# Recurrent convolution read from PSUM, separate counts for its two readers, and statistics products at other places

## What is computed

```
x_new = layer_norm(DEEPNORM_ALPHA * x + gate[:, None] * y, ln_g, ln_b)
...
h = rms_norm(x, g_mix_pre[l])
z = h @ w_in[l]
...
# rg_lru_branch(xb, gb): xb = u_rx, gb = u_rg, both 1024 x 1024 columns of z
xc = causal_dwconv(xb, conv_w, conv_b)            # 4 taps, per channel
gates = einsum('bshi,ghij->gbshj', xh, w_gates)   # 16 heads of 64, two gates
r, i = sigmoid(gates[0]), sigmoid(gates[1])
a = exp(-LRU_C * r * softplus(-lru_lambda))
u = sqrt(1 - a*a) * i * xc
h[t] = a[t] * h[t-1] + u[t]                       # over the tokens
out = h * gelu(gb)
```

## Time and profile before

| | us |
|---|---|
| median of 3 timed runs (3225.26 to 3228.08) | 3226.74 |
| the profiled execution | 3221.17 |
| its span, first to last instruction | 3219.0 |
| PE busy | 3083.0 |
| DVE, ACT, POOL busy | 1525.1, 749.5, 1187.0 |

### The profile page before, as it was taken

One profiled execution on the slowest core, in us unless ns is written; L12 is line 12 of the kernel. 1 busy time (PEld: TensorE's weight loads), 2 busy tenths in 40 slices (PEclk: granted clock), 3 DMA queues, 4 the chain that ended last, 5 costly groups with the idle time before them and its releaser, 6 DMA issues.

```text
span 3219.0 us, 40660 instructions
## 1 busy us (share of the span) xinstructions
PE 3083.0 (96%) x16864; PEld 2493.3 (77%) x16864; DVE 1525.1 (47%) x1728; ACT 749.5 (23%) x995; POOL 1187.0 (37%) x553
## 2 busy tenths in 40 slices
PE   6999998999999999899988999999899999999998
PEld 5877876788877787787666788788688888888877
DVE  3134418528643324835666602443664155155477
ACT  2011215312231123512444411112211001001132
POOL 2232220126643232047553344353244344443442
PEclk9999999999999999999999999999999999999999
DMA  6210111333231011213411111112211111111211
GB/s 245 72 33 8 35 41 48 112 127 120 72 128 33 14 41 48 73 52 105 137 53 33 40 46 51 40 53 103 77 47 46 53 46 52 46 46 52 106 44 72
DMA packets 64283, 213.39 MB, mean 66 GB/s; under 512 B 6160, under 2 KB 7952, under 8 KB 64144
## 3 DMA queue, kind: packets, MB, share of 16 engines
q1 hardware_dynamic: 44256, 149.97, 14.2%
q10 hardware_dynamic: 19888, 61.39, 5.2%
HBM read 194.56 MB, written 16.78 MB: 66 GB/s over the span
## 4 chain that ended last, share of the span: by engine, by line
PE 65%; issue 13%; DVE 11%; POOL 6%; DMA 3%; ACT 2%; POOLq 0%; SPq 0%; DVEq 0%; ACTq 0%
PE ps L586 57%; DVE Sb L2033 3%; POOL w_hi L506 3%; DMA raw<-s 3%; POOL w_lo L508 3%; PE ps L897 2%; DVE C L2353 1%; PE ps L807 1%; PE ps L722 1%; PE ps L813 0%; DVE g_lo L2435 0%; PE ps L1109 0%; PE ps L829 0%; PE ps L784 0%; DVE st L2035 0%
## 5 line engine op out<-in xcount | busy, mean ns | idle before, releaser
L506 POOL TENSOR_TENSOR w_hi<-raw,pool_zero 128x1024 fp32r<-128x1024 f32 (+2 forms) x256 | 485.1, 1895 | 1936.6 <-PE ps L586 1798.3
L508 POOL TENSOR_TENSOR w_lo<-raw,w_hi 128x1024 fp32r<-128x1024 f32 (+2 forms) x256 | 667.1, 2606 | 20.1
L586 PE MATMUL ps<-g_hi,w_hi 128*128 128x512 f32 x1632 | 535.4, 399 | 27.3 <-ACT xb L1261 11.1
L586 PE MATMUL ps<-g_lo,w_hi 128*128 128x512 f32 x1632 | 524.7, 393 | 0.0
L586 PE MATMUL ps<-g_hi,w_lo 128*128 128x512 f32 x1632 | 524.3, 392 | 0.0
L586 PE MATMUL ps<-h_hi,w_hi 128*128 128x512 f32 (+1 forms) x1496 | 429.0, 378 | 6.6 <-POOL w_lo L508 4.6
L586 PE MATMUL ps<-h_lo,w_hi 128*128 128x512 f32 (+1 forms) x1496 | 409.5, 365 | 0.0
L586 PE MATMUL ps<-h_hi,w_lo 128*128 128x512 f32 (+1 forms) x1496 | 409.1, 365 | 0.0
L586 PEld LDWEIGHTS ps<-g_hi,w_hi 128*128 128x128 f32 x1632 | 308.9, 190 | 105.6 <-ACT xb L1261 12.8
L586 PEld LDWEIGHTS ps<-g_hi,w_lo 128*128 128x128 f32 x1632 | 309.7, 190 | 65.5
L586 PEld LDWEIGHTS ps<-g_lo,w_hi 128*128 128x128 f32 x1632 | 309.5, 190 | 65.7 <-issue 1.2
(11 more groups left out here) (353 smaller groups left out, 3538.0 us busy)
## 6 DMA issues: line engine op xcount, KB each, us to landing
raw<-s SPq DMA_DIRECT2D x239, 512.0 KB, 3.4
modring<-modw ACTq DMA_DIRECT2D x32, 512.0 KB, 4.7
modfirst<-modw SPq DMA_DIRECT2D x4, 1024.0 KB, 18.0
modfirst<-modw ACTq DMA_DIRECT2D x4, 1024.0 KB, 25.0
x_saved<-Y ACTq DMA_DIRECT2D x1, 4096.0 KB, 13.4
x_part<-x_saved ACTq DMA_DIRECT2D x2, 2048.0 KB, 9.6
x_saved<-Y ACTq DMA_DIRECT2D x2, 2048.0 KB, 8.9
B<-x_saved ACTq DMA_DIRECT2D x1, 4096.0 KB, 15.6
```

What stands on the lines that cost most here:

```text
L506: G.tensor_tensor(w_hi[s][:, :n], raw[s][:, :n], zero.to_broadcast([P, n]), ALU.add).then_inc(hi_done, 1)
L508: G.tensor_tensor(w_lo[s][:, :n], raw[s][:, :n], w_hi[s][:, :n].bitcast(F32), ALU.subtract)\
L586: last = T.matmul(ps[:, o + c0:o + c0 + size], wt[s][:, kk], xx[:, k, t0:t0 + size], start=(x == 0 and n == 0), stop=(x == k_n - 1 and n = ...
```

## The change

Seven edits:

1. `convolved(c)` for c = 0 and 3 to 7 reads the slab from PSUM banks 0 and 1: the newest tap first over all 1024 columns, then the three others on shifted, shorter views. Chunks 1 and 2 still go through `xb1` and `xb2`. `xb` and the copies into it are gone.
2. DVE's order is `gated_input(c)`, `recurred(c)`, `convolved(c + 2)`, `low(c)`.
3. GELU has its own semaphore `gelu_done`. In the recurrent branch an even slab waits for `rnn_xc` and an odd slab for `gelu_done` (argument `taken`) in place of the common count; `evac_done` jumps by 16 at the first gate of the mix to be in step again.
4. The first half of chunk 0's input stays in bank 0 (no `head(0)`), S0 goes to bank 1 beside it, S2 to bank 4; the six head slabs use banks 0, 3, 1, 3, 1, 3.
5. The gate maps stand at other places: those of chunk 0 after k-step 1 of S3 (4 before), of 1 after 0 of S6 (4), of 2 after 6 of S7 (1 of S8), of 3 after 5 of S9 (6), of 4 where they were (4 of S11), of 5 after 3 of S13 (2), of 6 after 3 of S15 (7 of S14), of 7 after 1 of M1 (4 of M0).
6. The statistics products stand at other k-steps.
7. `residual(h, 0)` writes its result to the sum in PSUM too, so that n = 1 adds to PSUM; `mix_inverse(0)` goes ahead of `residual(1, 5)`.

The core of the diff (left out: the declaration of the semaphore, the ACT order's full list):

```diff
+HEAD_BANK = [0, 3, 1, 3, 1, 3]
...
                 for n in range(KD):
                     slab(G_OUT_B + n, n % 2, g_hi, g_lo, KD, half[1], 3,
-                         between=at_points(n, 0, [(0, 2), (2, 6), (3, 3), (6, 2), (7, 1)]))
+                         between=at_points(n, 0, [(0, 2), (2, 2), (3, 0), (5, 5), (6, 2)]))
                 for c in range(R_HEAD):
                     slab(G_RHEAD + c, c % 2, g_hi, g_lo, KD, half[0], 3, SPLITS["h2a"] if c == 0 else None,
-                         between=at_points(c, 1, [(0, 5), (2, 7), (3, 4), (5, 5), (5, 7)]))
+                         between=at_points(c, 1, [(0, 4), (2, 6), (3, 2), (5, 4)]), bank=HEAD_BANK[c],
+                         freed=G_RHEAD + c - 2 if c > 1 else None)
+                mix_spread(1)
...
-            first_pair(G_RNN, g_hi, g_lo, "h2b", 2, segs=(half[1], half[1]), dead=2, freed=G_RNN - 1)
-            for c in range(2, R_HEAD):
-                slab(G_RNN + c, c % 2, g_hi, g_lo, KD, half[1], 2, between=rnn_gate_maps(0, 4) if c == 3 else None)
-            gate_maps_in = {6: (1, 4), 8: (2, 1), 9: (3, 6), 11: (4, 4), 13: (5, 2), 14: (6, 7)}
+            first_pair(G_RNN, g_hi, g_lo, "h2b", 2, segs=([(512, 512, 512)], half[1]), dead=3, freed=G_RNN - 1)
+            slab(G_RNN + 2, 0, g_hi, g_lo, KD, half[1], 2, freed=G_RNN - 1, bank=4)
+            slab(G_RNN + 3, 1, g_hi, g_lo, KD, half[1], 2, between=rnn_gate_maps(0, 1), taken=(gelu_done, 1))
+            slab(G_RNN + 4, 0, g_hi, g_lo, KD, half[1], 2, taken=(rnn_xc, 1))
+            slab(G_RNN + 5, 1, g_hi, g_lo, KD, half[1], 2, taken=(gelu_done, 2))
+            gate_maps_in = {6: (1, 0), 7: (2, 6), 9: (3, 5), 11: (4, 4), 13: (5, 3), 15: (6, 3)}
             for c in range(R_HEAD, 16):
                 slab(G_RNN + c, c % 2, g_hi, g_lo, KD, SEC, 2,
-                     between=rnn_gate_maps(*gate_maps_in[c]) if c in gate_maps_in else None)
+                     between=rnn_gate_maps(*gate_maps_in[c]) if c in gate_maps_in else None,
+                     taken=(gelu_done, c // 2) if c % 2 else (rnn_xc, c // 2) if c > 6 else (evac_done, G_RNN + 1))
             for j in range(4):
-                slab(G_RMIX + 4 * j, 0, g_hi, g_lo, KD, SEC, 2, between=rnn_gate_maps(7, 4) if j == 0 else None)
-                slab(G_RMIX + 4 * j + 1, 1, g_hi, g_lo, KD, SEC, 2)
+                slab(G_RMIX + 4 * j, 0, g_hi, g_lo, KD, SEC, 2, taken=(rnn_xc, 8) if j == 0 else None)
+                slab(G_RMIX + 4 * j + 1, 1, g_hi, g_lo, KD, SEC, 2, between=rnn_gate_maps(7, 1) if j == 0 else None,
+                     taken=(gelu_done, 8) if j == 0 else None)
...
+            gelu(0)
+            rest(1, 4)
             act.wait_ge(xs_out, 48)
             gate_acts(0)
-            rest(3)
+            gelu(1)
             rnn_root(0)
-            rest(4)
-            rest(5)
+            rest(2, 0)
+            gelu(2)
             for c in range(1, 8):
-                if c > 2:
-                    evac(G_RNN + 2 * c + 1, gelus[c % 2], SEQ, 2, ACT.Gelu_apprx_tanh)
                 rnn_high(c - 1)
+                if c == 7:
+                    mix_gate(G_RMIX, 0, 0)
                 gate_acts(c)
-                if 3 <= c < 7:
-                    next_input(c + 1)
+                if 2 <= c < 7:
+                    gelu(c + 1)
                 rnn_root(c)
-                if c == 1:
-                    next_input(3)
...
+                    total = ps[:, SUM * BANK:(SUM + 1) * BANK]
+                    if n == 0:
+                        own.link(V.scalar_tensor_tensor(total, ps[:, o:o + 512], mod[:, 40, 0:1], x_part[h][:, 0, :],
+                                                        ALU.mult, ALU.add))
...
+                dve.wait_ge(slab_done, G_RNN + 2 * c + 1)
+                own.link(V.tensor_scalar(xc, ps[:, 0:SEQ], tap(3), vcol("rconvb", c), ALU.mult, ALU.add))
+                for sh in (1, 2):
+                    own.link(V.scalar_tensor_tensor(xc[:, sh:], ps[:, 0:SEQ - sh], tap(3 - sh), xc[:, sh:], ALU.mult, ALU.add))
+                V.scalar_tensor_tensor(xc[:, 3:], ps[:, 0:SEQ - 3], tap(0), xc[:, 3:], ALU.mult, ALU.add).then_inc(rnn_xc, 1)
...
             for c in range(8):
                 gated_input(c)
-                if c < 7:
-                    convolved(c + 1)
                 recurred(c)
+                if c + 2 < 8:
+                    convolved(c + 2)
+                low(c)
```

More of the change, by code:

```diff
@@ L572, in slab @@
                     pe.wait_ge(evac_done, freed)
+                elif taken is not None:
+                    pe.wait_ge(*taken)
                 elif not first:
@@ L1697, in mix_gate @@
                     act.wait_ge(mix_used, first + n - 1)
-                evac(g0 + 4 * (n // 2) + n % 2, T2[:, n % 2, :], SEQ, 2, ACT.Sigmoid)
+                evac(g0 + 4 * (n // 2) + n % 2, T2[:, n % 2, :], SEQ, 2, ACT.Sigmoid,
+                     count=G_RMIX - G_RNN if g0 == G_RMIX and n == 0 else 1)
+            gelu(0)
+            rest(1, 4)
+            act.wait_ge(xs_out, 48)
+            gate_acts(0)
+            gelu(1)
+            rnn_root(0)
+            rest(2, 0)
+            gelu(2)
+            for c in range(1, 8):
+                rnn_high(c - 1)
+                if c == 7:
+                    mix_gate(G_RMIX, 0, 0)
+                gate_acts(c)
+                if 2 <= c < 7:
+                    gelu(c + 1)
+                rnn_root(c)
             def mix_value(g0, n):
```

82 lines of the change are left out of this document (39 added, 43 removed).

## The result

The changed kernel takes **3189.96 us** (median of four runs, 3189.13 to 3192.21) against 3226.00 for the kernel before on the same chip: a ratio of 0.9889, 95% interval 0.9872 to 0.9907, 36.0 us by the medians. The forecast was 3188.7. The profiled executions differ by less: 3221.17 before, 3190.06 now, 31.1 us.

A forecast was written before the change was run, and what follows sets the result against it. PE was taken as the bound, losing time to waits and slow clock. Gains of 31.8 us in the branch and 6.3 before it, from 3221.2, gave 3183.1; plus 5.6 for the timed median, 3188.7 us, range 3177 to 3206.

The forecast's parts named there:

- What bounds the kernel: PE, busy 3083.0 of 3219.0 us; gains come from its 136 us idle and its time at the lower clock.
- The length of the branch without waits: PE from S3 to M2: slabs and eight gate maps at 3.03 us need 171.1 us, where the trace has 210.3.
- The steady chunk: Recurrent branch after the change: a chunk's recurrence has a period of some 18 us, under PE's 24.8.
- The three kinds of wait: PE's branch waits for input copies (11.1 us), GELU (6.0) and, before gate maps, `rnn_xc` (5.3); all were to go.
- The spare of 5 to 9 us: Even slabs for chunks 2 to 5: PE arrives 29.2 to 33.3 us after the maps, the convolution ends after 24.0.
- The price of the convolution: DVE's four operations from PSUM take 1.27 us each, 5.1 together, also beside POOL's work.
- The start of the branch: S3 1 us earlier; S5 waits 0.4, S8 about 4 (bounds 0 and 13), then slow clock costing 2.
- The end of the branch: M2's last k-step: the last split is ready after 20.3 to 22 us, so PE waits 2 us, from 0 to 5.
- The front: End of the second layer, up to the recurrent branch's first pair: 6.3 us gained, between 4 and 8.
- No contention: Rival: no waits before S8 and M2 and no slow stretch, 7.7 us more gained, 3181 us; chance 0.2.
- repeated lag: Rival: contention of 9 to 11 us a chunk makes S8, S10 and S12 wait, with slow stretches, 3203 us; chance 0.2.
- The slower rival: Rival: all recurrence and PSUM operations contended, a chain of 43 us, 30.5 us a chunk, 3243 us; chance 0.04.

The follow-up runs named there:

- the best kernel: Changed kernel with convolutions 3 to 7 from an SBUF copy, PE waiting only for it, earlier gate maps 6 and 7, later first mix gate: 3174.94 us, 0.9862.
- the run with eight repeats: Changed kernel plus eight repeats of the recurrence's last product on DVE in each of chunks 2 to 5, ahead of the convolution: 3212.67 us, ratio 0.9978.

## Why the prediction came out right, and where it was not

**What bounds the kernel.** Right: all of the gain came from PE's idle time and slow clock in the stretches that the earlier trace rows shows, and the waits of the earlier trace rows are the ones that went.

**The length of the branch without waits** is the first mis-sized term. I took 171.1 us from S3 to M2, with 3.03 for each gate map, from the map's start to the next slab matmul in the earlier trace rows. But that matmul is itself a slow one. The same place in the trace of before, one row further, and a map in the changed kernel:

```profile
1736.74 1.03 PE L586 MATMUL ps<-g_hi,w_hi 128*128 128x512 f32 x2
1737.61 0.61 PE L586 MATMUL ps<-g_lo,w_hi 128*128 128x512 f32 x2
```

```profile
1656.77 3.60 PE L1117 MATMUL ps<-B,rgwt 128*128 128x512 f32 x8
1659.80 1.03 PE L590 MATMUL ps<-g_hi,w_hi 128*128 128x512 f32 x2
1660.67 0.61 PE L590 MATMUL ps<-g_lo,w_hi 128*128 128x512 f32 x2
```

The pair behind a map takes 0.87 us from start to start instead of 0.45: a map costs 3.45, eight of them 3.4 us more. In the prediction I had these 3.4 in hand, as "the other 4 are spread over matmuls around the gaps", and counted them as gained. They are no part of any gap. With them the floor is 174.5, and the branch of the best kernel, whose waits are gone, confirms it: 195.01 from the first pair, of which the part up to S3 was 20.10 in the changed kernel, leaves 174.9. I had named 176 to 180 us from S3 to M2 as a sign of being right; it took 182.04.

**The steady chunk** was right. The three kinds of wait are gone, the clock is at 1.00 behind S8, and ACT waits for the maps where the maps used to wait, as at chunk 3:

```profile
1691.40 1.12 ACT L1662 ACTIVATE B<-ps,vec 128x1024 f32<-128x1024 f32 x1 [10.38 <-PE ps L1117]
```

The spare of 5 to 9 us stands in the trace as 8.8, 5.4, 5.8 and 5.8 from the end of a convolution to the even slab that waits for it (S10, S12, S14 and M0). Its size was right and its course was not: I had it grow from 5.2 to 9.3. The first is large since S8's wait lies in it, and in the later chunks two or three operations are stretched (of chunk 4, 1.22 us to 3.30 and to 2.73). The runs with more work show it from the other side: four products a chunk, which add the 3.7 us by which they are stretched to their own 4.9, brought waits of up to 1.6, eight, in 13.7 us, brought 3.2 to 6.1. One correction: the spare by the trace is less than what can be added, as the convolution itself sometimes waits for its slab (1.2 us at chunk 4).

**The price of the convolution.** 5.2 us for four against 5.1. `TENSOR_SCALAR` from PSUM is 1.33 to 1.345 us, a little outside my bounds of 0.81 and 1.27, which cost nothing. That PSUM sources are not slowed beside POOL holds for all of the 18 operations that met it, and the SBUF source shows the alternative: 8.2 us. By the Trainium skill (VectorE: DVE Perf Modes, Why PSUM operands drop a tier) the first tap would lose its double rate; the trace agrees, 1.33 against 0.81. By the Trainium skill (SBUF — State Buffer, Who interferes with whom) a VectorE operation with at most one SBUF input, outside the two-port modes, does not contend with GpSimd, and one with two SBUF inputs does with a GpSimd operation that reads SBUF; both runs agree, the PSUM source with at most 1.345 us, the SBUF source with 3.25.

**The start of the branch.** S3 starts 20.10 us behind the first pair instead of 21.10, the one microsecond foreseen. S5 and S6 did not wait (0.7 expected). S8 waited 4.23 for 3.7, and its slow clock cost 2.8 for 2. The trace has the mechanism as I put it: chunk 0's chain with five operations stretched beside POOL's splits, 8.5 us more than undisturbed, in DVE's timeline of the changed kernel,

```profile
1625.03 2.38 DVE L2399 TENSOR_TENSOR B<-B 128x1024 f32<-128x1024 f32 x1 [3.59 <-ACT B L1666]
1627.45 2.92 DVE L2400 SCALAR_TENSOR_TENSOR B<-B 128x1024 f32<-128x1024 f32 x1
1630.30 3.42 DVE L2401 TENSOR_TENSOR B<-B 128x1024 f32<-128x1024 f32 x1
...
1633.88 2.67 DVE L2406 TENSOR_TENSOR B<-B 128x1024 f32<-128x1024 f32 x1
1636.59 4.34 DVE L2407 TENSOR_TENSOR_SCAN B<-B 128x1024 f32<-128x1024 f32 x1
```

one more in chunk 1, then the convolution of chunk 3 in front of PE. What I missed is that it need not stand in front of PE: an early copy would have freed the banks.

**The end of the branch.** M2 waited 3.06, for 2 with bounds 0 and 5: the last split was ready 24.3 us after the start of maps 7, not 20.3 to 22, since two operations of chunk 7 were stretched (2.92 and 3.17 us for 1.22 each) where I had allowed for one. And the stretch at 1.2 GHz behind it, 1.7 us, was missing from the sum, though the start of the branch had one for a wait of like length. Together 4.8 for 2.

So the branch gained 1.0 + 28.3 - 4.8 = 24.5, not 31.8: 3.4 from the maps, 2.8 at M2, 1.3 at S8 less 0.7 at S5 and S6, and 0.5 in small pieces.

**The front** gained 7.0 in these two traces, for 6.3. That hit is partly the clock's. Against the old front at full clock it is 4.2, at the low edge of my 4 to 8. Counted from slab 96 the mean comes 3.7 us earlier (47.29 against 51.01 us behind it; 4.4 foreseen) and waited 2.55 (2.3). From the mean to the first pair it is 36.3 us against 36.8 at full clock: 0.5 where I had 1.9, so the moved products of the second half bought almost nothing.

**The offset.** The working ended at 3183.1 for a profiled execution, 7 us too low, and I added 5.6 because the timed median of before stood so far above its profiled run. The changed kernel's median stands 0.1 below its own. So 3188.7 met 3189.96 with two errors of opposite sign, and that it came so near is luck. Against the trace the gain was too large by 7.0, and that is the error to learn from.

**The rivals.** "No contention" fell with S8's wait, "repeated lag" with the full clock behind S8, and POOL's weights held up one slab, S2, for 1.8 us (2.1 before). The slower rival did not come about, and the run with eight repeats tests its working: most of the branch's gain (25 of 29 us) was lost with 13.7 us more on the chain. The formula (chain plus 17 to 18 us, for two chunks) gives 30.6 us a chunk for the chain of 43.8; the maps of chunk 3 and those of chunk 7 are 121.0 us apart there, 30.3 a chunk.

## What to carry to other kernels

Ask of each wait for a buffer which is the earliest event that frees it. With the convolution from an SBUF copy, letting PE wait for the copy and not for the convolution saved 10 us by that alone. The direct read from PSUM is worth 2.8 us as long as PE waits for the convolution, but it holds the banks longer: the copy that frees them early, in spite of its slower operations, beats it by 7.1. Before an instruction is delayed because "no one waits", follow every in-order queue behind its readers: moving one convolution took 4.2 us from one slab and gave 7.5 to the next, by way of a GELU. And when a sum of ideal times leaves an unexplained rest, look at the rows on both sides of the special operations before counting it as gain: the rest may be their price.
